# Stage ends of a two-block network on one core: post norms by half rows, gla's squares on ScalarE, a store in four pieces

## What is computed

```
def rms_norm(x, g):
    y = xf * lax.rsqrt(jnp.mean(xf * xf, axis=-1, keepdims=True) + EPS)
    return (y * g.astype(jnp.float32)).astype(x.dtype)

# gla, last lines: o is (tokens, 4 heads, 256)
    o = rms_norm(o, o_norm_g).reshape(B, S, GLA_V).astype(h.dtype) * jax.nn.silu(g)
    return o @ w_out

# second block, last lines of the mixer and of the feed-forward
        x = x + gt_m * rms_norm_2(mix, g_post_mix[layer])
        fx = swiglu(modulate(rms_norm_2(x, g_pre_ffn[layer]), sh_f, sc_f), w_ffn_in[layer], w_ffn_out[layer])
        x = x + gt_f * rms_norm_2(fx, g_post_ffn[layer])
```

## Time and profile before

| | |
|---|---|
| median of 3 runs | 1485.23 us (1482.4 to 1488.07) |
| profiled execution, its own time | 1486.92 us |
| its span, first to last instruction | 1485.1 us |
| TensorE busy | 1425.4 us (96%) |
| VectorE, ScalarE, GpSimd busy | 65%, 49%, 10% |
| HBM traffic | 171 GB/s over the span |

### The profile page before, as it was taken

The page is one execution under the profiler, slowest core; times in us unless marked ns, Lnnn a source line. Parts: engine busy times, 40 slices in busy tenths (PEclk is TensorE's granted clock), DMA queues, the critical chain, the costliest instruction groups (busy, mean ns, idle before and its releaser), DMA issues.

```text
span 1485.1 us, 20000 instructions
## 1 busy us (share of the span) xinstructions
PE 1425.4 (96%) x8348; PEld 1246.6 (84%) x8348; DVE 968.4 (65%) x1067; ACT 723.1 (49%) x914; POOL 154.4 (10%) x177
## 2 busy tenths in 40 slices
PE   6999999899999999999999889999999999899996
PEld 5888898897888888888899768888878778788885
DVE  5788867774667765767666756566656755565553
ACT  5454446452544444544455655454445455454442
POOL 2000011760000002000012012000023002000000
PEclk9999999999999999999999999999999999999998
DMA  8877534332576668976545316555534102265551
GB/s 264 285 255 258 181 116 140 114 114 66 207 265 239 245 199 187 326 253 240 188 141 173 117 48 226 192 198 171 178 101 133 54 4 85 79 209 195 198 181 47
DMA packets 175448, 255.15 MB, mean 172 GB/s; under 512 B 4659, under 2 KB 153438, under 8 KB 172286
## 3 DMA queue, kind: packets, MB, share of 16 engines
q1 hardware_dynamic: 173264, 248.62, 50.1%
q0 software_dynamic: 1904, 5.19, 1.8%
q10 hardware_dynamic: 190, 0.06, 0.0%
HBM read 252.54 MB, written 1.31 MB: 171 GB/s over the span
## 4 chain that ended last, share of the span: by engine, by line
PE 90%; DVE 5%; ACT 2%; issue 1%; POOL 1%; SPq 0%; DMA 0%; DVEq 0%; POOLq 0%; ACTq 0%
PE banks L586 26%; PE banks L606 14%; PE acc L182 9%; PE acc L183 9%; PE acc L184 9%; PE banks L182 4%; PE banks L183 4%; PE banks L184 4%; PE acc L1031 2%; PE banks L2203 1%; PE acc L2177 1%; DVE w_lo L162 1%; PE acc L1041 1%; PE banks L2254 1%; DVE arena L1200 1%
## 5 line engine op out<-in xcount | busy, mean ns | idle before, releaser
L162 DVE TENSOR_TENSOR w_lo<-w_raw,w_hi 128x2048 fp32r<-128x2048 f32 x212 | 489.3, 2309 | 169.0 <-ACT w_hi L156 168.1
L156 ACT ACTIVATE w_hi<-w_raw 128x2048 fp32r<-128x2048 f32 x212 | 404.3, 1908 | 67.2 <-PE acc L184 34.0
L586 PE MATMUL banks<-h_both,w_hi 128*128 128x512 f32 x1680 | 415.2, 394 | 3.1 <-DVE h_both L298 1.6
L586 PEld LDWEIGHTS banks<-h_both,w_hi 128*128 128x128 f32 x1680 | 311.0, 190 | 66.1 <-issue 5.6
L606 PEld LDWEIGHTS banks<-h_both,w_lo 128*128 128x128 f32 x1680 | 215.4, 191 | 8.2
L606 PE MATMUL banks<-h_both,w_lo 128*128 128x256 f32 x1680 | 217.9, 283 | 0.0
L182 PE MATMUL acc<-w_hi,act_hi 128*128 128x512 f32 x408 | 158.9, 389 | 0.7 <-issue 0.7
L183 PE MATMUL acc<-w_lo,act_hi 128*128 128x512 f32 x408 | 159.1, 390 | 0.0
L184 PE MATMUL acc<-w_hi,act_lo 128*128 128x512 f32 x408 | 158.9, 390 | 0.0
L182 PE MATMUL banks<-w_hi,h_both 128*128 128x256 f32 x432 | 126.0, 292 | 0.0
L183 PE MATMUL banks<-w_lo,h_both 128*128 128x256 f32 x432 | 123.2, 285 | 0.0
(11 more groups left out here) (319 smaller groups left out, 1886.1 us busy)
## 6 DMA issues: line engine op xcount, KB each, us to landing
w_raw<-in_ffn_w_gu SPq DMA_DIRECT2D x88, 1024.0 KB, 5.1
w_raw<-in_ffn_w_down SPq DMA_DIRECT2D x44, 1024.0 KB, 4.8
arena<-in_w_ada SPq DMA_DIRECT2D x24, 1024.0 KB, 5.2
w_raw<-in_w_ffn_in SPq DMA_DIRECT2D x22, 1024.0 KB, 5.1
w_raw<-in_gla_w_in SPq DMA_DIRECT2D x12, 1024.0 KB, 5.3
w_raw<-in_diff_w_in SPq DMA_DIRECT2D x12, 1024.0 KB, 5.2
w_raw<-in_w_ffn_out SPq DMA_DIRECT2D x11, 1024.0 KB, 4.8
w_raw<-in_w_in SPq DMA_DIRECT2D x9, 1024.0 KB, 5.2
```

What stands on the lines that cost most here:

```text
L156: eng.activation(w_hi[:, slot, :], w_raw[:, slot, :], ACT.Copy).then_inc(sem("unit_hi"), 1)
L162: eng.tensor_tensor(w_lo[:, slot, :], w_raw[:, slot, :], w_hi[:, slot, :].bitcast(F32), ALU.subtract).then_inc(sem("unit_split"), 1)
L586: return pe.matmul(outs[ct], hi[:, k, ct * P:(ct + 1) * P], h_both[:, k, :, t], start=k == 0, stop=k == KT - 1)
```

## The change

1. Post norms: the squares are taken by half rows, each as its quarter of `acc` is done, and into `xn` instead of `post_t`. GpSimd makes an rstd for each tile, in two steps of the mean (the first half's part, then the sum) as the norms already do. VectorE multiplies `acc` by the gate row before the rstd is known, a quarter at a time, and one operation on each half row then multiplies by rstd and adds to `x_sb`. The order on VectorE is written out: products of (0,0), (0,1), (1,0), additions of tile 0, product of (1,1), additions of tile 1.
2. The norm of ffn4 thus works by half rows too (`halved`).
3. The store: four transfers of a tile's half row, each as it is added.
4. gla: the split of unit 15 stands behind the last two copies of scores; all eight squares are ScalarE's, and TensorE tells of every second head.
5. mix: the fcol matmuls stand behind the scores of heads 0 and 1, ScalarE's copy behind the exponentials of head 0.

```
         def halved(name):
-            return index[name] > 0 and stages[index[name] - 1] not in POST_STAGES
+            return index[name] > 0
...
-            eng.wait_ge(sem("gla_out"), 1)
-            for h in range(GH):
-                eng.activation(gla_gap[:, 0, ...], acc[:, 0, ...], ACT.Square, accum_out=ssq[:, h:h + 1])
+            for t in range(TT):
+                for h in range(GH):
+                    if h % 2 == 0:
+                        eng.wait_ge(sem("gla_out"), 2 * t + h // 2 + 1)
+                    n = GH * t + h
+                    eng.activation(gla_gap[:, t, ...], acc[:, t, ...], ACT.Square, accum_out=ssq[:, n:n + 1])
...
-                split_lo(eng, u + 8 + p)
+                if p < GLEVELS - 1:
+                    split_lo(eng, u + 8 + p)
                 kept(2 * p)
                 kept(2 * p + 1)
-            eng.wait_ge(sem("gla_out"), 2)
-            for h in range(GH):
-                square_sum(eng, acc[:, 1, ...], gla_gap[:, 1, ...], ssq[:, GH + h:GH + h + 1])
+            split_lo(eng, u + 7 + GLEVELS)
...
+        def post_pool(pool, name):
+            for t in range(TT):
+                first = 4 * posts_before(name) + 2 * t
+                part, total = mean_sq[:, 58 + t:59 + t], mean_sq[:, t:t + 1]
+                pool.wait_ge(sem("post_squares"), first + 1)
+                pool.tensor_scalar(part, ssq[:, 56 + 2 * t:57 + 2 * t], 1.0 / D, EPS, ALU.mult, ALU.add)
+                mean_wait(pool)
+                pool.wait_ge(sem("post_squares"), first + 2)
+                pool.tensor_scalar(total, ssq[:, 57 + 2 * t:58 + 2 * t], 1.0 / D, part, ALU.mult, ALU.add)
+                mean_wait(pool)
+                pool.tensor_tensor(rstd[:, t:t + 1], total, minus_half[:, t:t + 1], ALU.pow)
...
         def post_scalar(eng, name):
             for t in range(TT):
-                eng.activation(post_t[:, t, :], acc[:, t, :], ACT.Square, accum_out=ssq[:, t:t + 1])
+                for half in range(2):
+                    c = post_quarter(eng, name, t, half)
+                    n = 56 + 2 * t + half
+                    eng.activation(xn[:, t, c], acc[:, t, c], ACT.Square, accum_out=ssq[:, n:n + 1])
...
-            for t in range(TT):
-                eng.scalar_tensor_tensor(post_t[:, t, :], acc[:, t, :], rstd[:, t:t + 1], gate_row[:, which, :],
-                                         ALU.mult, ALU.mult)
-            for t in range(TT):
-                eng.wait_ge(sem("post_scaled"), 2 * k + t + 1)
-                eng.tensor_tensor(x_sb[:, t, :], x_sb[:, t, :], post_t[:, t, :], ALU.add)
+            def gated(t, half):
+                c = post_quarter(eng, name, t, half)
+                eng.wait_ge(sem("post_squares"), 4 * k + 2 * t + half + 1)
+                eng.tensor_tensor(post_t[:, t, c], acc[:, t, c], gate_row[:, which, c], ALU.mult)
+            def added(t):
+                eng.wait_ge(sem("post_rstd"), 2 * k + t + 1)
+                eng.wait_ge(sem("post_gated"), 4 * k + 2 * t + 2)
+                for half in range(2):
+                    c = slice(half * 512, half * 512 + 512)
+                    eng.scalar_tensor_tensor(x_sb[:, t, c], post_t[:, t, c], rstd[:, t:t + 1], x_sb[:, t, c], ALU.mult,
+                                             ALU.add)
+            gated(0, 0)
            gated(0, 1)
            gated(1, 0)
            added(0)
            gated(1, 1)
            added(1)
...
-            sp.dma_start(out.rearrange("b (t p) d -> p (b t) d", p=P), x_sb[:, :, :]).then_inc(sem("stored"), 16)
+            for t in range(TT):
+                for half in range(2):
+                    sp.wait_ge(sem("x_updated" if half else "x_half_updated"), done)
+                    c = slice(half * 512, half * 512 + 512)
+                    sp.dma_start(rows_out[:, t, c], x_sb[:, t, c]).then_inc(sem("stored"), 16)
```

More of the change, by code:

```diff
@@ L922, in gla_pool @@
                 pool.tensor_tensor(rstd[:, c], mean_sq[:, c], minus_half[:, c], ALU.pow).then_inc(sem("gla_rstd"), 1)
[L924 to L937 removed]
+        def post_pool(pool, name):
[3 more added lines that the diff above has]
+                pool.wait_ge(sem("post_squares"), first + 1)
+                pool.tensor_scalar(part, ssq[:, 56 + 2 * t:57 + 2 * t], 1.0 / D, EPS, ALU.mult, ALU.add)\
+                    .then_inc(sem("mean_ready"), 1)
+                mean_wait(pool)
+                pool.wait_ge(sem("post_squares"), first + 2)
+                pool.tensor_scalar(total, ssq[:, 57 + 2 * t:58 + 2 * t], 1.0 / D, part, ALU.mult, ALU.add)\
+                    .then_inc(sem("mean_ready"), 1)
+                mean_wait(pool)
+                pool.tensor_tensor(rstd[:, t:t + 1], total, minus_half[:, t:t + 1], ALU.pow)\
+                    .then_inc(sem("post_rstd"), 1)
         def mixers_before(name):
@@ L1807, in mix_scalar @@
             exps(0)
+            eng.wait_ge(sem("ml_fcol"), 1)
+            keep("fcol", st[:, 64:96], bank[2][:, 0:32])
             exps(1)
@@ L2280, in mix_tensor @@
             value_tile(0)
+            pe.wait_ge(sem("att_k_ready"), 1)
+            pe.wait_ge(sem("att_q_ready"), 2)
+            pe.wait_ge(sem("mix_copied"), copied("mq"))
+            scores(0)
+            scores(1)
             pe.wait_ge(sem("ml_g_ready"), 4)
```

78 lines of the change are left out of this document (30 added, 48 removed).

## The result

The changed kernel takes 1478.12 us (median of 20 runs, 1472.6 to 1484.11) beside 1486.15 for the kernel before in the same runs; ratio 0.9937, 95% interval 0.9918 to 0.9956 (intervals further down are of the same kind). It is faster by 0.6%, a little more than a measurement here can tell from no change, and about half of the forecast: 1478 lies outside the range of 1464 to 1476. Two later sets of the same kernel gave 1477.31 and 1478.84; over all three, 37 executions, the mean is 1478.2 with a standard error of 0.4.

A forecast was written before the change was run, and what follows sets the result against it. TensorE, 90% of the chain, was taken as the bound, so edits pay only where it waits or at the end. Terms 6.05 + 0.85 + 3.7 + 3.5 + 1.95 = 16.05 gave 1470.9 profiled, 1469.2 median, range 1464 to 1476.

The forecast's parts named there:

- Gla, 6.05: Gated linear attention's tail: output product released earlier 3.0, its clock at full rate 1.9, squares on ScalarE 1.15 us.
- The rival in which the clock of the product stays low: Gla's output product still runs at the low clock; loses 1.9 us, giving 1471.1; chance 0.12.
- End of mix, 3.7: Post norm and ffn4's norm at mix's end: L280 earlier by 3.7 us, between sums of 3.3 and 4.5.
- The blocked case: End of mix: each pool operation starting under a VectorE addition waits for it; gain 3.3 us.
- End of the program, 3.5: Last post norm, same shape as mix's end: additions end 3.4 to 3.7 us earlier, taken as 3.5.
- the store, 1.95: Final store in four pieces: the last carries a quarter, taking 0.65 instead of 2.6 us; gain 1.95.
- The rival with a fixed 4.4 for each store piece: Stage ends gain little: store pieces cost 4.4 us each and fcol's gain is absorbed; 1472.0; chance 0.10.
- fcol, 0.85: Mix, first attention heads: fcol behind the scores closes TensorE's idle time before the transposes; gain 0.85 us, bounds 0 and 1.87.
- slower through the clock: With other gaps, TensorE falls to the low clock in more stages; result 1493 us; chance 0.02.
- another rival: Gla product's clock stays low, since low stretches also stand where TensorE was busy with little; 1471.1; chance 0.12.

The follow-up runs named there:

- the eight matmuls: Changed kernel with eight unused identity matmuls between the scores and fcol; two sets, 12 executions, mean 1471.2 us, ratios 0.9853 and 0.9890.
- the kernel with fcol back: Changed kernel with only the fcol matmuls and their copy put back ahead of the scores; 18 executions, mean 1475.5 us, median 1472.9.
- the matmuls behind fcol: Changed kernel with eight unused identity matmuls between fcol and the first transposes; 1477.5 us.

## Why the prediction was right or wrong

The forecast was 1469.2; the median 1478.1. Point by point:

- *Gla, 6.05*: right, 5.95 measured, in all three parts: wait 0.94, clock 1.00, warming matmuls as the last wait. The rival in which the clock of the product stays low didn't happen: in the three profiles without the gla change it is low there, in none of the 17 with it (one of them has a short low stretch behind the transposes). The same tail takes 17.85 us in all of these but the ones with 12 warming matmuls (16.7).
- *End of mix, 3.7*: mechanism right, size off: 3.24. The blocked case (3.3) was worked out and then only half believed; the row of the longer split already had the same operand kind. The wait under L278 was in neither sum.
- *End of the program, 3.5, and the store, 1.95*: 3.3 and 1.98. The rival with a fixed 4.4 for each store piece is refuted: from the last addition, which releases the last piece, it is 2.46 to the span's end.
- *fcol, 0.85*: the failed step. The sentence "TensorE now does scores, fcol, then the transposes with no gap, at 1152.3 instead of 1153.16: gain 0.85" priced the order at the full clock. At the full clock it is right: from the end of value tile 0 to the end of head 0's value matmuls the kernel before takes 1.87 + 12.38 = 14.25, and the profile with the eight matmuls 15.28 - 1.98 = 13.30, a gain of 0.95. But the clock falls, and the changed kernel takes 18.0 for it, in each of its three profiles: 3.8 lost in place of 0.85 gained. What the term lacked is the clock under the new order. When it falls with fcol ahead (the second profile of the kernel before) it takes 1.87 + 17.90 = 19.8, so the old order pays more, but only in some executions.
- *The rival "slower through the clock"* named what went wrong, more time at the low level, though it blamed "other gaps" and not the order of small matmuls; it had a chance of 0.02 and was put aside with "The change makes gaps shorter only, which speaks against it". That sentence took idle time for the only cause. The same prediction had noted, under another rival, that low stretches also stand where TensorE is busy with little. Stretches that fall cost about 0.4 us for each us at the low level (mix takes 196.2 with 34 us of them in the changed kernel, 183.6 with none in the second profile with the eight matmuls).

In sum: 14.5 of 15.2 us arrived in the profile. Its execution was forecast at 1470.9 and took 1477.1. The 6.2 between them are 0.7 at the stage ends, 4.65 at the heads (0.85 and 3.8), 5.1 behind the heads and 0.25 more around the span (2.1 where 1.8 was to stay), less the 4.5 won by low stretches elsewhere, which is luck. The number also started from too low a base: the three executions shown had the median 1485.23, the 109 of the kernel before in all sets have the median 1487.1 and the mean 1489.7 (one more, of 3599 us, is left out). By ratio of means the changed kernel is at 1478.2 / 1489.7 = 0.992, and the kernel with fcol back at 0.990; the forecast without the fcol term is 1470.05 / 1485.23 = 0.990. So the terms other than fcol came out whole within the noise of such a ratio (about 0.003), and some 2 to 4 us of the missed 9 are the base. What is shown: behind the scores fcol brought the low stretch at the heads in every profile (5 of 5, against 4 of 11 ahead of them), and full matmuls between the scores and fcol took it away (0 of 4). What stays open: which property of the small matmuls lets the clock fall, and what makes the stretch at 1206 to 1227, and the ones in gla, come or not in executions of one and the same kernel. Of the 8.9 us lost in the profile 3.8 are from the heads and 5.1 from behind them, and how much of these 5.1 the change causes isn't settled.

The best versions beat both kernels: eight matmuls ahead of fcol (two sets, 12 executions, mean 1471.2, 0.9853 and 0.9890), and fcol ahead of value tile 0 with value tile 1 behind the scores and 12 warming matmuls (6 executions, mean 1471.2, 0.9873, interval 0.9839 to 0.9908). They are the best of many versions with few executions each, so a new set may well come out higher: the eight matmuls with 12 warming ones, expected at 1468 to 1469, came to 1475.0.

## What to carry to other kernels

Before an order on TensorE is priced, mark in the granted clock what runs there: a row of small matmuls with nothing full between them is a place where the clock may fall although the engine is never idle, and closing an idle gap by lining more of them up can cost more than the gap. Full matmuls between them are the remedy to try, best ones that have to be done anyway; here these kept the clock up in their one profile, while a gain in time is shown for the useless ones alone. And where executions of one kernel fall into groups, a single profile or a median of a few can't price an edit of a few us: count how many executions lie in each group.

## What the hardware showed that was not expected

- The granted clock went from 1.00 to 0.50, the 1.2 GHz level, with TensorE busy 4.00 of 4.00 us shortly before (window 1137 to 1141 of the changed kernel, where it fell at 1141.9) and 2.00 of 2.00 (window 1143 to 1145 with the matmuls behind fcol, where it fell at 1145.6). The Trainium skill ("TensorE: Matmul & The Clock Gate", Part 1: The HAM clock gate) says that the gate follows how busy TensorE has been; by busy time alone it should not have fallen here, and the measurement decides. The page also says that the point at which the clock rises behind a kernel's first matmuls varies from run to run of one kernel. These traces show such a variation in the middle of a kernel (mix took 190.6 and 200.3 in two profiles of the kernel before, with 11.6 and 37.1 us at the low level).
- A 128x1 GpSimd operation took 0.71 beside a 512-column addition of VectorE and 0.27 with none beside it, so the wait can cost more than the operation's own work. Beside a gate product with one input in PSUM it took 0.27 too, and beside L278, 1024 columns with one SBUF tensor as input, another one took 0.75.
- The span ended 2.46 us behind the last write of the data where a 256 KB piece was stored last from SP's queue, 4.44 where it was 1 MB.
